# Routing for a mixture of experts: tiles chosen while the projection runs, logits with tokens on partitions

## The reference

```python
for i in range(DEPTH):
    hn = rms_norm(h, norm1_g[i])
    h = h + (rwkv7_time_mix(hn, ...) if i % 2 == 0 else conformer_conv(hn, ...))   # both end in a product with a 1024 x 1024 matrix
    hn = rms_norm(h, norm2_g[i])
    h = h + hierarchical_moe(hn, ...)
return rms_norm(h, final_g)

def hierarchical_moe(h, w_group, b_group, w_expert, b_expert, w_gate, w_up, w_down):
    gp = softmax(ht @ w_group + b_group)                     # 4 groups
    p_top, g_idx = top_k(gp, 1)
    el = (ht @ w_expert + b_expert).reshape(-1, 4, 8)        # 8 experts in each
    top_l, e_idx = top_k(el[chosen group], 2)
    w_in = softmax(top_l) * p_top
    y = sum over the 32 experts of gate[e] * ((silu(ht @ wg[e]) * (ht @ wu[e])) @ wd[e])
```

## Time and profile before

| | |
|---|---|
| median of 3 runs | 1217.81 us (1216.09 to 1220.73) |
| profiled execution | 1218.87 us, of which 1217.1 us lie between its first and last instruction (the span) |
| PE busy | 1144.6 us, 94% of the span |
| PE weight loads | 627.2 us, 52% |
| DVE, ACT, POOL busy | 529.2, 425.1, 205.6 us |
| chain that ended last | PE 79%, DMA 12%, DVE 3%, ACT 2% |
| DMA | 281.97 MB, mean 232 GB/s |

### The profile page before, as it was taken

The page is one execution under the profiler, slowest core; times in us unless marked ns, Lnnn a source line. Parts: engine busy times, 40 slices in busy tenths (PEclk is TensorE's granted clock), DMA queues, the critical chain, the costliest instruction groups (busy, mean ns, idle before and its releaser), DMA issues.

```text
span 1217.1 us, 29462 instructions
## 1 busy us (share of the span) xinstructions
PE 1144.6 (94%) x12520; PEld 627.2 (52%) x12520; DVE 529.2 (43%) x1004; ACT 425.1 (35%) x823; POOL 205.6 (17%) x234
## 2 busy tenths in 40 slices
PE   6999999999999989999998889999999999998785
PEld 5365555555555644555554445544554555554442
DVE  6756464664555510511111125899941511111125
ACT  5345354454454421321121124555443321111123
POOL 2000000000000000222222110688800112221110
PEclk9999999999999999999999999999999999999998
DMA  4017311011011258799999998126702889999996
GB/s 162 3 55 297 116 56 41 20 59 42 20 59 49 98 201 339 283 354 421 423 420 423 424 379 344 70 71 253 316 1 75 324 304 422 422 423 422 422 401 256
DMA packets 53779, 281.97 MB, mean 232 GB/s; under 512 B 14956, under 2 KB 17132, under 8 KB 36496
## 3 DMA queue, kind: packets, MB, share of 16 engines
q1 hardware_dynamic: 43952, 263.73, 54.1%
q0 software_dynamic: 9408, 16.32, 3.7%
q10 hardware_dynamic: 288, 0.03, 0.0%
HBM read 265.84 MB, written 30.41 MB: 243 GB/s over the span
## 4 chain that ended last, share of the span: by engine, by line
PE 79%; DMA 12%; DVE 3%; ACT 2%; issue 2%; SPq 1%; DVEq 0%; ACTq 0%
PE psum L1609 15%; PE psum L974 14%; PE psum L2143 9%; PE psum L2441 8%; PE psum L1790 6%; PE psum L987 6%; DMA h<-rows 5%; DMA big<-in_moe_w_gate_up_dram 4%; DMA h<-in_moe_w_gate_up_dram 4%; PE psum L941 2%; PE psum L1914 1%; PE psum L1779 1%; SPq L423 1%; PE psum L2451 1%; PE psum L2417 1%
## 5 line engine op out<-in xcount | busy, mean ns | idle before, releaser
L974 PE MATMUL psum<-big 128*64 128x256 f32 x1536 | 188.4, 388 | 24.0 <-issue 13.2
L1609 PE MATMUL psum<-big 128*128 128x512 f32 x384 | 192.8, 623 | 1.4 <-ACT big L1660 0.2
L974 PEld LDWEIGHTS psum<-big 128*64 128x64 f32 x1536 | 107.0, 138 | 92.2 <-issue 33.1
L1108 DVE SCALAR_TENSOR_TENSOR big<-psum,big 128x128 f32<-128x128 f32 x64 | 22.4, 351 | 292.2 <-ACT big L1058 292.2
L987 PE MATMUL psum<-big 128*64 128x512 f32 x512 | 121.0, 593 | 1.1 <-DMA big<-in_moe_w_down_dram 0.8
L2143 PE MATMUL psum<-big 128*128 128x512 f32 x256 | 115.6, 604 | 0.8 <-ACT big L2544 0.8
L894 POOL DMA_INDIRECT chosen<-big x60 | 59.9, 998 | 312.3 <-ACT big L1069 150.7
L1983 ACT COPY big<-psum 128x512 f32<-128x512 f32 (+1 forms) x112 | 69.1, 649 | 109.8 <-PE psum L1790 107.4
L2386 POOL TENSOR_TENSOR big<-big 128x512 f32<-128x512 f32 x76 | 96.7, 1272 | 36.0 <-ACT big L2526 25.5
L1790 PEld LDWEIGHTS psum<-big 64*64 64x64 f32 x4096 | 71.5, 134 | 49.3 <-issue 48.5
L2441 PE MATMUL psum<-big,conv_w 128*128 128x512 f32 x224 | 96.5, 592 | 0.0
(11 more groups left out here) (290 smaller groups left out, 1395.2 us busy)
## 6 DMA issues: line engine op xcount, KB each, us to landing
big<-in_moe_w_gate_up_dram SPq DMA_DIRECT2D x40, 2048.0 KB, 31.1
big<-in_moe_w_down_dram SPq DMA_DIRECT2D x64, 1024.0 KB, 27.7
conv_w<-in_moe_w_gate_up_dram SPq DMA_DIRECT2D x8, 2048.0 KB, 31.6
h<-in_moe_w_gate_up_dram SPq DMA_DIRECT2D x8, 2048.0 KB, 26.6
big<-in_moe_w_gate_up_dram SPq DMA_DIRECT2D x16, 1024.0 KB, 12.3
big<-in_rwkv_w_rkv_dram SPq DMA_DIRECT2D x24, 512.0 KB, 4.2
chosen<-h SPq DMA_DIRECT2D x8, 1024.0 KB, 12.6
conv_w<-in_conv_w_pw_dram SPq DMA_DIRECT2D x8, 1024.0 KB, 4.8
```

What stands on the lines that cost most here:

```text
L974: last = nc.tensor.matmul(o[half * SLOTS:(half + 1) * SLOTS, 0:F_EXP].rearrange("p (u f) -> p u f", u=2), m.xT[e // 2 % 2][:, c, (e % 2) * ...
L1609: last = nc.tensor.matmul(bank[b], m.w[:, n, c, :], x[:, c, :], start=(c == 0), stop=(c == C - 1))
```

## The change

It has four parts.

1. **Logits.** `pe_logits` now takes the tokens as the stationary operand, one tile at a time, and the 36 columns stream. The logits come with tokens on partitions, so the copies and `pe_flip_logits` are gone. Logits of tiles 0 and 1 are computed inside the projection, behind chunk 3 of tile 3; transposes of tile 2 behind chunk 6 of tile 3; logits of tile 2 directly behind the projection.
2. **Choice.** `choose_experts` runs through to the one-hot matrices and the codes, for tiles 0 and 1 together, then for 2 and for 3 alone. VectorE chooses tiles 0 and 1 before it adds tile 2. Indices are compared as they are (u32), without casts.
3. **Slots.** The rounds are counted before the one-hot matrices `hot` are made; these are made in four pairs instead of eight singles.
4. **Tables.** A token's number is coded with an offset (`NO_TOKEN`, 1024), so that `gather_at` is one addition and comes first in `dve_tables`.

Besides, `pe_stay_busy` is issued two times instead of five ahead of the ranks and two times instead of four ahead of the experts, and banks and counts of the semaphore steps change to suit.

```diff
-        NORM_BANKS = ((6, 7), (2, 3)) * 2
+        NORM_BANKS = ((6, 7), (2, 3), (2, 3), (0, 1))
...
+            st.done(nc.gpsimd.iota(token_low[:, 2:3], pattern=[[1, 1]], base=0, channel_multiplier=1,
...
+            nc.gpsimd.iota(token_high[:, 1, :], pattern=[[P, TT]], base=-NO_TOKEN, channel_multiplier=0,
...
+        LOGIT_BANK = (6, 7, 2, 0)
+        def pe_logits(m, pe, t):
+            if t == 0:
+                pe.wait_ge(m.router_scaled.sem, m.router_scaled.by(1))
             for c in range(C):
+                if c in (0, C // 2):
+                    pe.wait_ge(m.hnT_ready.sem, m.hnT_ready.by(2 * t + (1 if c == 0 else 2)))
+                last = nc.tensor.matmul(bank[LOGIT_BANK[t]][:, 0:N_LOGITS], m.hnT[:, c, t * P:(t + 1) * P],
+                                        m.w_route[:, c, :], start=(c == 0), stop=(c == C - 1))
+            last.then_inc(m.logits_in_psum.sem, 1)
+        def pe_route_last(m, pe):
+            pe_logits(m, pe, TT - 2)
             pe_norm_columns(m, pe, TT - 1)
+            pe_logits(m, pe, TT - 1)
...
             for t in range(2):
                 square(t)
                 root(t)
+            for t in range(2):
+                columns(t)
+            act_low_codes(m, act, 0, 2)
+            for t in range(2, TT):
+                square(t)
+                columns(t)
+                root(t)
             act.wait_ge(m.squares.sem, m.squares.by(TT))
+            act.wait_ge(m.logits_in_psum.sem, m.logits_in_psum.by(TT))
...
+            dve_mixed(mixer, dve, 1)
+            dve_mean_square(m, dve, 1)
+            dve.wait_ge(consts_ready, 2)
+            step(nc.vector.memset(m.logits[:, :, n:], -3.0e38))
+            choose_experts(0, 2)
+            dve_mixed(mixer, dve, 2)
+            dve_mean_square(m, dve, 2)
+            dve_mixed(mixer, dve, 3)
+            choose_experts(2, 3, meanwhile=lambda: dve_mean_square(m, dve, 3))
+            choose_experts(3, 4)
...
+        def dve_slots(m, dve):
+            for t in range(TT):
+                nc.vector.tensor_tensor(m.hot[:, 2 * t:2 * t + 2, :], slot_of_col[:].unsqueeze(1).broadcast_to([P, 2, P]),
+                                        m.rank[:, t, :].unsqueeze(2).broadcast_to([P, 2, P]), ALU.is_equal
+                                        ).then_inc(m.hot_ready, 1)
...
+                mine = token[p].rearrange("p (g b) -> p g b", b=2)[:, :, half]
+                last = nc.vector.tensor_scalar(m.gather_at[p].bitcast(i32), mine, float(NO_TOKEN), None, ALU.add)
...
-                pe_stay_busy(m, 4)
+                pe_stay_busy(m, 2)
...
                     for c in group:
                         add(t, c)
+                        if t == TT - 1 and c == LOGITS_BEHIND:
+                            for u in range(2):
+                                pe_logits(after, pe, u)
+                        if t == TT - 1 and c == C - 2:
+                            pe_norm_columns(after, pe, 2)
```

More of the change, by code:

```diff
@@ L561, in pe_logits @@
             for c in range(C):
[L562 to L576, removed]
@@ L685, in choose_experts @@
-                for t in two:
+                step(nc.vector.tensor_tensor(m.in_group[:, tiles, :],
+                                             group_iota[:].unsqueeze(1).broadcast_to([P, count, N_EXP]),
+                                             m.gidx[:, tiles, 0:1].bitcast(u32).broadcast_to([P, count, N_EXP]),
+                                             ALU.not_equal))
+                step(nc.vector.scalar_tensor_tensor(out=m.el[:, tiles, :], in0=m.in_group[:, tiles, :], scalar=-3.0e38,
+                                                    in1=m.logits[:, tiles, 0:N_EXP], op0=ALU.mult, op1=ALU.add))
@@ L686, in choose_experts @@
+                if meanwhile:
+                    meanwhile()
+                for t in range(first, end):
                     last = nc.vector.max(m.emax[:, t, :], m.el[:, t, :])
                 step(last)
-                for t in two:
+                for t in range(first, end):
                     last = nc.vector.max_index(m.eidx[:, t, :].bitcast(u32), m.emax[:, t, :], m.el[:, t, :])
                 step(last)
-            for pair in range(2):
-                choose_experts(pair)
-            step(nc.vector.tensor_copy(m.eidx_f, m.eidx[:, :, 0:2].bitcast(u32)))
@@ new lines, in choose_experts @@
+                step(last)
+                step(nc.vector.tensor_tensor(m.picks[:, tiles, :], m.pick[:, tiles, 0, :], m.pick[:, tiles, 1, :], ALU.add))
+                assert st.n == PICKED[end]
+                for i in range(2):
+                    last = nc.vector.tensor_tensor(rhs[:, tiles, :, 2 + i, :], m.pick[:, tiles],
+                                                   token_high[:, i, tiles].unsqueeze(2).unsqueeze(3)
+                                                   .broadcast_to([P, count, 2, N_EXP]), ALU.mult)
@@ new lines, in choose_experts @@
+                coded = st.done(last)
+                assert end < TT or coded == CODED
+            if m.layer == 0:
+                dve.wait_ge(chosen_finite.sem, chosen_finite.by(FINITE_STORED))
+            dve_mixed(mixer, dve, 0)
+            dve.wait_ge(m.params_in.sem, m.params_in.by(16 * m.n_params))
+            nc.vector.tensor_tensor(m.w_route, m.w_route, m.g_col.unsqueeze(2).broadcast_to([P, C, N_LOGITS]),
+                                    ALU.mult).then_inc(m.router_scaled.sem, 1)
```

192 lines of the change are left out of this document (63 added, 129 removed).

## The result

The changed kernel takes 1228.35 us (median of 5 runs, 1227.59 to 1229.97), the kernel before 1220.73 us in the runs beside it (5 runs, 1216.09 to 1222.34). The ratio is 1.0069, 95% interval [1.0053, 1.0086]: slower, by 8.4 us (the two medians lie 7.6 apart). The prediction said 1218.4 with a range up to 1226. The profiled execution has a span of 1225.9 us against 1217.1, and a mean granted clock of 0.982 against 0.991.

What follows compares the result with a forecast made beforehand. It took the routing chain from projection to first expert as the bound, then the weight stream; 2 x (-0.6) + 1.8 = +0.6 us gave 1219.5 for the profiled execution, 1218.4 as the median, range 1211.5 to 1226.

Steps and rivals of the forecast that it cites:

- Ahead of the projection's end: Two tiles' logits (1.75 us each) and tile 2's transposes (0.90) delay the projection's end by 4.4 us per layer.
- first and second rival: Logits passes cost only their stream: 1212.6 us, chance 0.13; or load and stream added: 1222 us, chance 0.08.
- Picks: Tile 3's expert picks done 7.45 us behind the projection's end instead of 11.51: -4.05 us per layer.
- Picks to gather table: Stretch from picks to gather table takes 3.95 us instead of 4.89: -0.95 per layer; one-hot pairs 1.45, bounds 1.2 and 1.7.
- own sum: Per layer, projection, picks and table steps together, before the gather: +4.4 - 4.05 - 0.95 = -0.6 us.
- What the gather meets: Delayed loads overlap the first gather by about 0.5 and 2 us, costing +0.3 in layer 0, +1.5 in layer 1.
- the clock falls at the gather: Fewer fillers leave PE idle before rows land, so its clock drops: +3.4 us over both layers, 1221.8; chance 0.12.
- The granted clock of 1.00 up to the first expert: Expected in the profile: TensorE's granted clock stays at 1.00 until the first expert's matmuls.
- The end follows the first expert: A shift of the first expert's start passes to the expert stage's end nearly one for one.
- My own sign of being wrong: First expert starting over 3 us earlier or later in either layer, or the end not following it.
- the gather collides: First gather lands in 10.7 us, as under the full stream, in both layers: +11.6 us, 1229; chance 0.12.

Runs made afterwards that it cites:

- e2: Changed kernel with the logits of tiles 0 and 1 behind chunk 5 of tile 3 instead of chunk 3; ratio to the kernel before 1.0052.
- e5: Changed kernel with the load into h held until the layer's first gather has landed; ratio to the kernel before 1.0014.
- e3: Kernel before with one wait more, holding the burst of loads until three tiles are added; ratio to the kernel before 1.0078.
- e9: Changed kernel with the load into h held until the first gather has landed and four fillers instead of two; ratio to the kernel before 1.0035.
- e6: Changed kernel with logits of tiles 0 and 1 behind chunk 5, load into h held until the first gather landed, and four fillers; ratio to before 1.0029.
- e1: Changed kernel with four fillers instead of two ahead of the first gathered rows; ratio to the kernel before 1.0061.
- e4: Kernel before with two fillers instead of four ahead of the first gathered rows; ratio to the kernel before 0.9995.
- e7: Kernel before with only rounds ahead of the slots, paired one-hot matrices and the gather table in one addition; ratio 0.9994.
- e8: Kernel before with the burst held back until three tiles are added and the load into h held until the first gather landed; ratio 1.0003.

## Why the prediction was wrong

- **Ahead of the projection's end: right.** +4.49 and +4.46 (counted from A and B) for +4.4; 0.109 us a pass for 0.11. The first and second rival (a pass bound by its stream, or by the sum of both) fall. The Trainium skill, "TensorE: Matmul & The Clock Gate", section "LDWEIGHTS (loading the stationary operand)", gives 107 ns for 128 columns, and the trace agrees.
- **Picks: right.** 7.63 behind the projection's end for 7.45.
- **Picks to gather table: too hopeful.** 4.26 and 4.44 for 3.95. The four one-hot pairs (L760) took 1.43 together in layer 1, as priced (1.45), but 1.86 in layer 0, above my upper bound of 1.7: one of them took 831 ns, where the median of all is 417. In layer 1 it was the codes (L652), 0.81 for two instead of 0.36. The rows that grew lie beside the same three instructions of POOL (503.79 to 505.73 in layer 0, from 967.95 in layer 1):
```profile
L760 DVE TENSOR_TENSOR big<-slot_of_col,big x16: 411/417/831, 504.8 to 1190.5; 128x256 bf16<-128x256 f32 x16
...
504.81 1.86 DVE L760 TENSOR_TENSOR big<-slot_of_col,big 128x256 bf16<-128x256 f32 x4
...
503.79 1.94 POOL L829 TENSOR_TENSOR big<-big 128x256 bf16<-128x256 f32 x3 [2.41 <-DVE big L652]
```
In e2 and e5, where POOL is done before the pairs start, they take 1.43 in both layers. The prediction has no term for POOL beside VectorE; no run was made for it alone. With the picks, the own sum is +4.49 - 3.88 - 0.63 = 0.0 in layer 0 and +0.1 in layer 1, and not -0.6.
- **"What the gather meets" failed**, and carries most of the miss: +0.3 and +1.5 was the term. The landing took 1.6 and 3.5 longer, of which 1.6 and 3.2 reach PE, since before the fillers had kept it until 4.07 behind the issue in layer 1 (e3 lands 1.4 and 4.3 later without the rest of the change). I had the mechanism, the delay of the loads (3.5, measured 3.6) and the place, and took the price as the length of an overlap that I put at 0.5 and 2 us. Two things were wrong in it. I took the ring for full behind the loads around 484, and followed the first load and the row stores to the burst's end; but the last transfer, the 2 MB into h behind the stores, sets it. The loads filled the engines until about 511.5 in layer 0 and 977 in layer 1, and not until 510 and 972 (975.8 counting layer 1's late start). And I priced the overlap below its length, while the gather moved nothing in it. The Trainium skill, "DMA: Bandwidth & Descriptors", section "Queues, rings and completion order", has an engine take turns between the queues that have work; half the overlap as its cost, an estimate from that, would be 1.3 us in all on my lengths. The trace does not agree: 50 packets of the loads and none of the gather from 975 to 977, and 4.8 us reach PE. Why the gather gets no turn, no run shows.
- **The rival "the clock falls at the gather" is no rival: it follows.** I gave it 0.12 beside a gather that lands in time. The late gather makes the wait (1.99 and 4.35 us of PE idle), and the clock falls in both layers: 1.7 us in layer 0, and in layer 1 0.7 on gate_up and 0.5 on its start (of the 0.9 by which the transposes grew), together 2.9 for the 3.4 that I had priced. The size was nearly right, the independence wrong. The granted clock of 1.00 up to the first expert, which I also expected, failed in layer 0 already at 506.
- **The end follows the first expert: right.** In the changed kernel the first expert starts 1.50 later behind A and loses 1.69: 3.2, and A to B is +3.7; behind B 3.77 and 0.71: 4.5, for +5.0. My own sign of being wrong, a first expert over 3 us late, is met in layer 1.

Sum, in the profiled execution, as it reaches the end of the first expert's 32 passes: own terms -0.1 + 0.1, landings 1.6 + 3.2, clock 1.7 + 1.2 make 7.7 of 8.7 us; the other 1.0 comes behind them, half in each layer. The rival "the gather collides" named nearly the time (1229) and the sign, but by a landing of 10.7 us; the landings were 5.9 and 7.1, and the clock made up the rest. Nearly the right time by a rival whose landing did not happen is luck. What stays open is why the clock falls elsewhere: at the last logits (e2, e5, e9), 0.7 us of idle time ahead of them, in the projection (e6), where PE had not idled, and at the fillers (changed kernel, e1, e2, e4, e6, e7). A wait alone doesn't settle it either: behind 1.80 us of idle time the first expert of e2 ran at 2.4 GHz, and behind 1.81 that of e3 did not.

## What to carry to other kernels

Work that is moved into a stage delays all that this stage frees: follow every transfer queued behind the freed buffer to the *last* one, and ask what latency-bound transfer is then in flight. Holding that one big load until the small one has landed took 0.55% back (e5), and 0.75% where the same delay had been made by itself (e8). A wait of TensorE that grows is priced with the clock behind it, not beside it.

## What the runs showed of the hardware

- An indirect gather on quiet DMA engines moved its first packet 1.6 to 1.8 us behind its issue and landed in 3.5 to 4.3 (before, e5). While the last 2 MB of a burst of plain loads filled the engines it moved nothing: first packet about 3.0 and 3.8 us behind the issue in the changed kernel, 2.6 and 4.2 in e3, and landings of 5.7 to 7.9 us.
- The paired comparison on VectorE, 128x256 from two broadcast operands, took 417 ns in the median, as the product of the same width in the earlier trace rows (422). Beside three instructions of POOL one took 831 (changed kernel, layer 0; 829 to 831 in e1, e6 and e9); where POOL was done first (e2, e5) none took over 426.
- A clock at the lower level costs again what it delays: in layer 1 of e6 a row of fillers meant to keep it up began at half speed and then held up by 2.1 us the rows it waited for.
- The clock fell not only behind idle time. In e2 and e5 it fell to 1.2 GHz while PE ran passes of 36 columns (16 of them took 3.53 us instead of 1.98), in e6 right behind 32 such passes in the projection.
